# The sums behind an MLP in another order, the products with h in a bank of their own, and the next weight panel rounded in halves with its low part in quarters

## The reference

```python
    # end of first_block
    a = jnp.square(jax.nn.relu(u2 @ w_up[l]))
    h = h + rmsnorm(a @ w_down[l], norm_mlp_post[l])
    # start of second_block
    shift, scale, gate = adaln(c, w_ada_mix[i], b_ada_mix[i])
    h = rms_norm(x, norm_mix_w[i]) * (1.0 + scale) + shift   # x is the h above
    proj = h @ w_in[i]
```

## Time and profile before

| | |
|---|---|
| median of 3 runs | 1705.75 us (1705.33 to 1705.82) |
| the profiled execution's own time | 1704.91 us |
| its span in the profile | 1703.1 us |
| mean granted TensorE clock | 0.998 of full |
| PE busy | 1685.5 us |
| DVE, ACT, POOL busy | 874.3, 704.9, 797.6 us |

### The profile page before, as it was taken

The page is one execution under the profiler, slowest core; times in us unless marked ns, Lnnn a source line. Parts: engine busy times, 40 slices in busy tenths (PEclk is TensorE's granted clock), DMA queues, the critical chain, the costliest instruction groups (busy, mean ns, idle before and its releaser), DMA issues.

```text
span 1703.1 us, 21894 instructions
## 1 busy us (share of the span) xinstructions
PE 1685.5 (99%) x7971; PEld 1370.9 (80%) x7971; DVE 874.3 (51%) x1361; ACT 704.9 (41%) x975; POOL 797.6 (47%) x608
## 2 busy tenths in 40 slices
PE   9999999899999999999999999999999999999998
PEld 7777777688888888787878888788888888888887
DVE  6234374553616166798897878864445511101113
ACT  5333364431313133457464554784424422222232
POOL 2434344555545454633434434354445544654453
PEclk9999999999999999999999999999999999999999
DMA  5222232265636342233223232322223222332232
GB/s 186 99 74 74 74 111 74 77 224 178 220 117 228 117 173 99 75 125 124 78 99 120 99 123 75 100 98 78 96 83 115 75 99 99 124 127 95 99 124 100
DMA packets 32540, 193.84 MB, mean 114 GB/s; under 512 B 3648, under 2 KB 5696, under 8 KB 13792
## 3 DMA queue, kind: packets, MB, share of 16 engines
q1 hardware_dynamic: 25376, 158.89, 26.7%
q10 hardware_dynamic: 7104, 34.15, 5.7%
HBM read 190.86 MB, written 2.16 MB: 113 GB/s over the span
## 4 chain that ended last, share of the span: by engine, by line
PE 92%; DVE 2%; POOL 2%; issue 2%; DMA 1%; ACT 1%; SPq 0%; DVEq 0%; POOLq 0%
PE gemm_bank L487 24%; PE gemm_bank L494 24%; PE gemm_bank L488 24%; PE gemm_bank L541 4%; PE gemm_bank L525 4%; PE gemm_bank L534 3%; POOL w_lo L449 2%; PE gemm_bank L529 1%; PE aux_bank L915 1%; DMA w_raw<-weights_dram 1%; PE aux_bank L646 1%; PE aux_bank L920 1%; PE aux_bank L900 1%; POOL h L465 1%; PE aux_bank L672 1%
## 5 line engine op out<-in xcount | busy, mean ns | idle before, releaser
L449 POOL TENSOR_TENSOR w_lo<-w_raw,w_hi 128x512 fp32r<-128x512 f32 x580 | 771.1, 1361 | 884.5 <-ACT w_hi L1199 884.5
L487 PE MATMUL gemm_bank<-a_hi,w_hi 128*128 128x512 f32 x1024 | 408.9, 399 | 0.0
L488 PE MATMUL gemm_bank<-a_lo,w_hi 128*128 128x512 f32 x1024 | 399.4, 390 | 0.0
L1199 ACT ACTIVATE w_hi<-w_raw 128x2048 fp32r<-128x2048 f32 x146 | 278.5, 1907 | 184.1 <-PE gemm_bank L494 124.3
L487 PE MATMUL gemm_bank<-b_hi,w_hi 128*128 128x512 f32 x688 | 267.8, 389 | 0.0
L488 PE MATMUL gemm_bank<-b_lo,w_hi 128*128 128x512 f32 x688 | 267.7, 389 | 0.0
L494 PE MATMUL gemm_bank<-a_hi,w_lo 128*128 128x512 f32 x1024 | 258.6, 394 | 0.0
L487 PEld LDWEIGHTS gemm_bank<-a_hi,w_hi 128*128 128x128 f32 x1024 | 192.3, 188 | 44.3 <-issue 5.4
L494 PEld LDWEIGHTS gemm_bank<-a_hi,w_lo 128*128 128x128 f32 x1024 | 190.2, 188 | 44.9 <-issue 6.2
L488 PEld LDWEIGHTS gemm_bank<-a_lo,w_hi 128*128 128x128 f32 x1024 | 192.5, 188 | 40.1 <-issue 1.9
L2098 DVE SCALAR_TENSOR_TENSOR aux_bank<-scratch,gcol,aux_bank 128x511 f32<-128x511 f32 (+15 forms) x240 | 165.8, 734 | 14.2 <-ACT aux_bank L1425 11.9
(11 more groups left out here) (395 smaller groups left out, 2107.3 us busy)
## 6 DMA issues: line engine op xcount, KB each, us to landing
w_raw<-weights_dram SPq DMA_DIRECT2D x146, 1024.0 KB, 4.7
arena<-ada_dram ACTq DMA_DIRECT2D x32, 768.0 KB, 4.3
acc<-cum_rows ACTq DMA_DIRECT2D x8, 512.0 KB, 3.8
h<-x_t_dram SPq DMA_DIRECT2D x8, 256.0 KB, 6.0
row_b<-cum_rows ACTq DMA_DIRECT2D x4, 512.0 KB, 4.7
scratch<-cum_rows ACTq DMA_DIRECT2D x4, 512.0 KB, 4.3
out_t_dram<-a_raw SPq DMA_DIRECT2D x7, 256.0 KB, 2.2
w_raw<-weights_dram SPq DMA_DIRECT2D x4, 256.0 KB, 5.3
```

Of the source, the lines that this page charges most:

```text
L449: ins = pool.tensor_tensor(wlo[s][:, w], raw[s][:, w], whi[s][:, w].bitcast(F32), ALU.subtract)
L487: pe.matmul(gemm_bank[bank][:, :], whi[slot][:, w], hi[:, k, :], start=(n == 0), stop=False)
L488: pe.matmul(gemm_bank[bank][:, :], whi[slot][:, w], lo[:, k, :], start=False, stop=False)
L1199: act.activation(whi[panel % 2][:, :], raw[panel % 2][:, :], ACT.Copy).then_inc(w_hi_ready, 1)
```

## The change

Five edits, all at the seam:

1. **PE, the sums** (`sums_of_mlp`). The group of `sq_sum`, the group of `gained_sum`, then the group of `sq[:, 1]`, and `sum_done` is signalled there. The two groups with h (`cross_sum`, `cross`) come behind, in `mix_bank`, which is gemm_bank 3: `cross_sum` before `spread(3)`, `cross` behind it, with a semaphore `cross_done` of its own. The layout in `aux[0]` goes from three columns a block to two.
2. **PE, the filler**. The small transposes give way to full products (128 x 512) of P_DT's high weights: one behind the first group, one behind the third, four behind `cross`, five ahead of `first_three`. Since the first ones write `mix_bank`, PE waits for P_DT's high weights and for bank 3 ahead of the first group.
3. **DVE**. `added_part(0)` now stands ahead of the four later steps of the new sum, which wait for `cross_done`; `added_part(1)` stands ahead of the second inverse.
4. **ACT**. Panel P_GRP is rounded in two instructions of 1024 columns: one ahead of the square of chunk 7 (it waits for the transfer and for tile 119), one behind it.
5. **POOL**. P_GRP's low part is no longer made in one go: two quarters, additions 0 to 2, a quarter, additions 3 and 4, a quarter, additions 5 to 7. PE waits for the quarters one by one in `first_three`.

```diff
@@ gpsimd
-            panels_of(P_MLP // 2 + 1, P_DT // 2 + 1)
-            for k in range(KC):
+            panels_of(P_MLP // 2 + 1, P_DT // 2)
+            low_parts(P_DT // 2, 0)
+
+            def low_piece(q):
+                w = slice(q * PANEL // LOW_PIECES, (q + 1) * PANEL // LOW_PIECES)
+                slot = P_GRP % 2
+                ins = pool.tensor_tensor(wlo[slot][:, w], raw[slot][:, w], whi[slot][:, w].bitcast(F32), ALU.subtract)
+                ins.then_inc(first_low if q < LOW_PIECES - 1 else w_lo_ready, 1)
+
+            def add_step(k):
                 pool.wait_ge(post_step, KC + k + 1)
                 pool.tensor_tensor(h[:, k, :], h[:, k, :], step3[k % 3], ALU.add).then_inc(h_ready, 1)
+
+            pool.wait_ge(w_hi_ready, P_GRP + 1)
+            low_piece(0), low_piece(1)
+            add_step(0), add_step(1), add_step(2)
+            low_piece(2)
+            add_step(3), add_step(4)
+            low_piece(3)
+            add_step(5), add_step(6), add_step(7)
@@ tensor
-            sums_of_parts()
-            sums_of_last()
-            keep_busy(1, 3)
-            spread(3)
-            keep_busy(2, 5)
+            def keep_products(count):
+                for _ in range(count):
+                    pe.matmul(mix_bank[:, :], whi[P_DT % 2][:, 0:P], whi[P_DT % 2][:, 0:S], start=True, stop=True)
+
+            def sums_of_mlp():
+
+                pe.wait_ge(w_hi_ready, P_DT + 1)
+                pe.wait_ge(bank_free[(T_GRP + 2) % 4], (T_GRP + 2) // 4 + 1)
                 pe.wait_ge(sq_sum_step, 17)
+                token_part(aux[0], 0, 2, sq_sum, True, False)
+                keep_products(1)
                 pe.wait_ge(gained_step, KC - 2)
+                token_part(aux[0], 1, 2, gained_sum, False, False)
                 pe.wait_ge(ysq_ready, 16)
                 for j in range(QT):
-                    mm = pe.matmul(aux[0][:, 3 * j:3 * j + 2], sq[:, 1, j * P:(j + 1) * P], one_gain2[:, :],
+                    mm = pe.matmul(aux[0][:, 2 * j:2 * j + 2], sq[:, 1, j * P:(j + 1) * P], one_gain2[:, :],
                                    start=False, stop=(j == QT - 1), skip_group_check=True)
-                mm.then_inc(sum_done, 2)
+                mm.then_inc(sum_done, 1)
+                keep_products(1)
+                pe.wait_ge(cross_step, 2 * (KC - 2) + 1)
+                token_part(mix_bank, 0, 1, cross_sum, True, False)
+                spread(3)
+                pe.wait_ge(cross_step, 2 * (KC - 2) + 2)
+                token_part(mix_bank, 0, 1, cross, False, True).then_inc(cross_done, 1)
+                for _ in range(4):
+                    pe.matmul(aux[2][:, :], whi[P_DT % 2][:, 0:P], whi[P_DT % 2][:, 0:S], start=True, stop=True)
@@ scalar
+                    half = PANEL // 2
+                    if last and j == KC - 1:
+                        act.wait_ge(w_loaded[P_GRP % 2], 16 * (P_GRP // 2 + 1))
+                        act.wait_ge(tile_done, T_DT)
+                        act.activation(whi[P_GRP % 2][:, 0:half], raw[P_GRP % 2][:, 0:half], ACT.Copy)
...
+                    if last and j == KC - 1:
+                        act.activation(whi[P_GRP % 2][:, half:PANEL], raw[P_GRP % 2][:, half:PANEL], ACT.Copy) \
+                            .then_inc(w_hi_ready, 1)
@@ vector
+            dve.wait_ge(r_ready, 4)
+            added_part(0)
+            dve.wait_ge(cross_done, 1)
             dve.wait_ge(new_step, 1)
-            dve.scalar_tensor_tensor(new_sum, summed(2), 2.0, new_part[:, :], ALU.mult, ALU.add).then_inc(new_step, 1)
+            dve.scalar_tensor_tensor(new_sum, cross_all, 2.0, new_part[:, :], ALU.mult, ALU.add).then_inc(new_step, 1)
...
-            dve.wait_ge(r_ready, 4)
-            added_part(0)
-            inverse(4)
             added_part(1)
-            dve.wait_ge(early_sums, 1)
+            inverse(4)
             added_part(2)
```

More of the change, by code:

```diff
@@ L301, in build @@
         gained_step = sem("gained_step")
-        early_sums = sem("early_sums")
+        cross_done = sem("cross_done")
+        first_low = sem("first_low")
         new_step = sem("new_step")
@@ L372, in build @@
         SPARE = (T_END - 4) % 4
+        mix_bank = gemm_bank[(T_GRP + 2) % 4]
         def free_value(t):
@@ L782, in mlp, with token_part @@
                     tile(i, P_MLP + 4 + j // 2, T_MLP + 8 + j, 8, 16, wide(j), b_hi, b_lo, first=j % 2 == 0)
-            def sums_of_parts():
+            def keep_products(count):
+                for _ in range(count):
+                    pe.matmul(mix_bank[:, :], whi[P_DT % 2][:, 0:P], whi[P_DT % 2][:, 0:S], start=True, stop=True)
+            def token_part(bank, n, step, of, start, stop):
+                for j in range(QT):
+                    at = step * j + n
+                    mm = pe.matmul(bank[:, at:at + 1], of[:, j * P:(j + 1) * P], ones[:, 0:1],
+                                   start=(start and j == 0), stop=(stop and j == QT - 1), skip_group_check=True)
+                return mm
@@ L831, in first_three @@
                         pe.matmul(gemm_bank[t % 4][:, :], whi[panel % 2][:, w], a_hi[:, k, :], start=(k == 0), stop=False)
-                        if k == 0:
-                            pe.wait_ge(w_lo_ready, panel + 1)
+                        if panel == P_DT and k == 0:
+                            pe.wait_ge(w_lo_ready, P_DT + 1)
+                        elif panel == P_GRP and j == 0 and k % 2 == 0:
+                            if k < 6:
+                                pe.wait_ge(first_low, k // 2 + 1)
+                            else:
+                                pe.wait_ge(w_lo_ready, P_GRP + 1)
                         pe.matmul(gemm_bank[t % 4][:, :], wlo[panel % 2][:, w], a_hi[:, k, :], start=False, stop=False)
@@ L843, in first_three @@
                                 mm.then_inc(tile_done, 1)
-            keep_busy(0, 7)
+            for _ in range(5):
+                pe.matmul(aux[0][:, :], whi[P_DT % 2][:, 0:P], whi[P_DT % 2][:, 0:S], start=True, stop=True)
             first_three()
@@ L1370, in _ @@
             act.wait_ge(sum_done, 4)
-            act.activation(root[:, :], aux[0][:, 0:3 * QT].rearrange("p (j n) -> p j n", n=3)[:, :, 0], ACT.Sqrt,
+            act.activation(root[:, :], aux[0][:, 0:2 * QT].rearrange("p (j n) -> p j n", n=2)[:, :, 0], ACT.Sqrt,
                            bias=eps[:, 0:1], scale=1.0 / D).then_inc(root_ready, 1)
@@ L1552, in _ @@
             after(P_GATE, T_GATE)
-            roots(5, sum_done, 6, e=1)
+            roots(5, sum_done, 5, e=1)
             load_table(ACT.Silu)
@@ L1647, in _ @@
                     after(P_WOUT2 + k // 2, T_WOUT2 + k - 1)
-            roots(6, sum_done, 7)
+            roots(6, sum_done, 6)
             for k in range(KC):
@@ L2026, in _ @@
             dve.tensor_scalar(new_sum, new_sum, 0.0, None, ALU.max).then_inc(new_step, 1)
-            dve.wait_ge(r_ready, 4)
-            added_part(0)
+            added_part(1)
             inverse(4)
-            added_part(1)
-            dve.wait_ge(early_sums, 1)
             added_part(2)
```

17 lines of the change are left out of this document (6 added, 11 removed).

## The result

The changed kernel takes 1708.76 us (median of 20 runs, 1707.71 to 1711.4), the kernel before in the same series 1705.38: ratio 1.0018, 95% interval 1.0012 to 1.0024, which is 3.4 us or 0.18% slower. That lies in the range (1704.8 to 1709.5) and within the 0.2% of "no change", by a little; the forecast was 1707.6, and rival A's number was 1709.3.

What follows compares the result with a forecast made beforehand. The seam was taken as bound by POOL's additions, the last operand, `a_lo` and PE's last products. POOL's gaps outweigh its early start: 1.85 us on 1704.91 gives 1706.8, plus 0.8 for the median 1707.6 us; range 1704.8 to 1709.5.

Steps and rivals of the forecast that it cites:

- rival A: PE's sums and spread: clock falls all the same, 681.2 to 684.6, first added part 1.7 later; 1709.3 us, chance 0.2.
- a fall of the clock: Sign that the prediction is wrong: clock was to stay at 1.00 through 681 to 685 at the seam.
- Where the seam ends, and by whom: End of the seam: POOL's additions, last operand, eight `a_lo` (6.1 us to the last), then PE's 17 products, 4.16 us.
- PE's last stall: PE at the end of the seam: its last stall on `a_lo` was to be over 1 us.
- The wait on bank 3, 1.05 later: Head of PE's sums: first group waits for DVE's last addition, starting at about 678.05 instead of 677.00.
- The first root, 0.4 earlier: After PE's reordered sums: root at 681.3 instead of 681.73, with the two-column group taken at 1.08 us.
- The spread at full clock, 1.0 earlier: PE's first spread: full clock because two products stand between the groups; first `added_part` at 683.4 instead of 684.37.
- My argument against A: Seam ahead of the MLP: clock stayed at 1.00 through PE's idle microsecond; also, two full products now stand in the groups.
- The gaps on POOL, 1.9 and 0.4: POOL idle 1.9 us before addition 0 and 0.4 before addition 1, waiting for the added parts; 2.3 us together.
- Quarters inside the additions: POOL: two quarters that filled the gaps before now stand inside the additions; last addition at 697.2 instead of 695.34.
- Filler that costs nothing: PE: four products (about 1.0 us) hidden under the wait for rinv2, five (1.2) under `a_hi`; that cover 0.4 us thick.
- The sum, 1.85: Whole seam: POOL's last addition and the seam's end 1.85 us later, giving 1707.6 us as median.

Runs made afterwards that it cites:

- the changed kernel's second profile: The changed kernel, unchanged, run again beside the other kernels of the second series: 1709.02 us against 1705.64 for the kernel before.
- the fill: Changed kernel, wait on bank 3 kept, three full products into another bank issued ahead of it: 1708.62 us against 1705.83 for the kernel before.
- the control: The kernel before, unchanged, timed and profiled again: 1705.47 us against 1705.54, ratio interval 0.9990 to 1.0008.
- six products: Fastest kernel (POOL from the first half) with two products instead of one behind first and third groups, two more ahead of the spread: 1706.52 us.

## Why the prediction was right, and where its sizes were off

The number was in the range, but 1708.76 is nearer to rival A's 1709.3 than to the 1707.6 of the sum, and the prediction named a fall of the clock as a sign that it is wrong. The clock fell. Right were the place, the chain and the order of the waits, wrong was the clock. That it fell only at 683.4, and not ahead of the spread as A had it, is luck, and it kept the loss small: in the changed kernel's second profile it fell earlier and the seam is 0.5 us longer.

*Where the seam ends, and by whom.* Right. POOL's additions, the last operand, the eight `a_lo` and 17 products are the chain in the changed trace too, and the 6.1 us from the last addition to the last 17 products stand unchanged (20.89 to 27.03). PE's last stall wasn't over 1 us, as forecast, but 0.16 twice: PE started the three tiles so late that it came to `a_lo` nearly together with DVE.

*The wait on bank 3, 1.05 later.* Right in place and size: 1.04 from the table, and 1.36 as a time of its own. Not foreseen is that it is worth some 2.2 us inside the changed kernel (3.38 against 1.16). In the traces it is 0.5 or 1.05 (21.08 against 21.59 and 22.13), and a difference of two such medians is uncertain by more than a microsecond. Part of the excess may be the clock: the five series that have both the wait and the new order of the sums show mean clocks of 0.9948 to 0.9953, all others 0.9958 to 0.9964. Why is open; what the fill showed is that it is not PE's idleness.

*The first root, 0.4 earlier.* 0.6 earlier in the trace. The two-column group took 0.9 start to start, not 1.08.

*The spread at full clock, 1.0 earlier.* **This step failed.** I took it that two products among the groups keep the clock up. It fell all the same, 0.5 us into the spread, so the first added part came 0.6 earlier instead of 1.0. (About 0.15 of that is a slip of mine: I counted the spread as 1.0, start to start, where the added part waits for its end, 1.16.) The groups behind it paid: `cross_done` at 8.02 instead of 7.1, and with it the second added part 0.8 late. That is the mechanism of rival A at another place: it named 681.2 to 684.6 and a price of 1.7, and it was 683.4 to 690.2 and 0.9 up to POOL's last addition. My argument against A, the clock held at 1.00 through an idle microsecond at the seam ahead of the MLP, rested on one execution; in the control's the clock fell at that very seam at 322.2, and in the changed kernel's at 318.2. The Trainium skill, "TensorE: Matmul & The Clock Gate", section "Part 1: The HAM clock gate", says that the array's recent work decides. No run here contradicts it, and none shows how much work is enough: neither a filled wait nor six products made the clock stay.

*The gaps on POOL, 1.9 and 0.4.* 2.20 and 0.91. Right in place; the second is larger by the half microsecond that `cross` lost at half clock. *Quarters inside the additions:* right, and shown alone (+1.9) and undone (-1.15 once the wait was gone, by itself a hint, with 1.4 less in the trace).

*Filler that costs nothing.* Nearly right, by luck. The cover of the four products was the wait for the second inverse; they took 2.05 us at half clock instead of 1.0, and the second spread started at 687.74, where the inverse had been there since 687.6. That is 0.1 us, because the inverse was itself 0.8 late. The first `new_operand` at 11.76 instead of 9.9 is those 0.8, the 0.1, and 0.8 to 0.9 by which the second spread took longer at half clock. It didn't set the end here, since POOL was later still, but it was the next in line: with the quarters first POOL waited there for 1.0 to 1.2 us.

*The sum, 1.85.* In the traces 2.75, or 3.29 with the changed kernel's second profile, in the medians 3.4. The difference to the forecast is the clock's 0.9 in the first trace; the other 0.6 lies between executions. At the same mean clock the kernels still differ: over all series, executions whose mean is 0.996 have a median of 1706.2 with the kernel before (11 of them) and 1708.8 with the changed one (18), and those whose mean is 0.995 have 1705.7 (29) and 1708.8 (8). So of the 3.4 the order of the code holds 2.6 to 3.1 and the clock's mean 0.3 to 0.8. The seams above put the order lower, at 1.2 to 1.7 against the control, so how the loss is shared between the two is known only roughly.

## What to carry to other kernels

When an engine goes from one piece of work to the next without a gap, work moved from ahead of its chain into it is paid in full, unless the time that comes free ahead is used at once: ask what the engine will do in that time. A wait that a mere filler instruction brings along (here for the bank that it writes) is a wait like any other and holds everything behind it. A filler of long instructions is only free while they end before what they cover, at the slower of the two clocks: here four products filled 2.05 us instead of 1.0 and used up all their cover. And where two executions of one program differ by 1.6 us at the place of interest, one profile can't settle a term of that size.

## What the runs showed of the hardware

The granted clock of one program differs between executions: over 11 of the kernel before, from 0.993 (1707.94 us) to 0.998 (1705.15 and 1705.42). In all 14 profiled executions it fell once at this seam, and it stayed at half for 3.4 us (4 of them), 6.8 us (8) or 10.2 us (2); the same code had 3.4 in one execution and 6.8 in another. It fell while PE was in its groups of one or two columns or the spread behind them, in one kernel in the products just ahead of the spread. Around the seam ahead of the MLP it fell once or twice in 12 of the 14, for 3.4 us each time.

Products among the groups didn't keep it up. Without any it fell between 680.6 and 683.2 (five executions), with two to five between 680.8 and 683.6 (eight), with six at 683.9. What would keep it up is open.
